# A two-layer decoder trunk: the token mixers' attention, retention and decode rows laid between projection tiles and convolution taps

## The chip, the cores and the metric

The kernel runs on one core of a Trainium2 chip, in one launch for both layers. The metric is the device time in microseconds, the median of several executions of the same program, in float32 throughout.

## The reference

The input is one prompt of 512 tokens and eight decode groups of four tokens each, 544 rows of 1024 numbers. Each of the two layers does the following, with its own weights:

```
h = x @ w_in          # 11 chunks of 256 columns:
                      # ret q,k,v,gate | dil q,k,v | conv val,gate | sgu u,v
A = layer_norm_per_head(retention(rot(q), rot(k), v)) * silu(gate)
B = dilated attention(rot(q), rot(k), v)   # prompt: own rows;
                                           # samples: 1024 cached rows as well
C = silu(layer_norm(causal_conv31(val * sigmoid(gate))))
D = gelu(u) * (lower_triangular(W_s) @ layer_norm_per_group(gelu(v)))
x = LN(alpha * x + concat(A, B, C, D) @ w_out)
x = LN(alpha * x + top-2-of-8 experts in the best of 4 groups(x))
```

Beside the final rows it returns the new retention states, the keys and values, the rows of the convolution, and the normalised v rows. A, B, C and D depend only on `h`, and not on each other.

## The kernel before, in words

One program is written for each engine, in program order, and counters (semaphores) order the engines against each other: `E.need(name, n)` makes an engine wait until `name` has been counted n times in this layer, `E.done` counts it, and `E.link` makes an engine wait for its own instruction. What stands behind a wait on the same engine waits too.

A layer has two parts. The first part, called the mixers here, is computed from x in SBUF. TensorE turns x into xT (`turn_rows`, L507), 128 rows at a time. Then come eleven projection chunks (`chunk`, L531): each is five tiles of eight matmuls, written in turn to five PSUM banks, and ScalarE moves each tile to `h` (`proj_out`, L948), with a sigmoid, gelu or silu where the chunk wants one. The order of chunks before is VAL, GATE, U, V, RG, RQ, RK, RV, SQ, SK, SV. Between them VectorE does the group norm of V (L1054) and the convolution, 62 instructions of 784 columns over a context that TensorE turned (L1103, L1106), then its norm. GpSimd multiplies VAL by GATE and rotates RQ, RK, SQ and SK (`rotate`, L1580), tile by tile and each operation by itself.

Only when all chunks are out are the queries and keys turned (L613, L617): eight groups of four transposes into xT, which x no longer needs. Then come the retention of the prompt in four steps (scores L635, products L642, rows L657 and L660, with a state in SBUF between the steps), the retention of the samples (L672 to L691), and 16 attention units (four row blocks of four heads). A unit is scores (L703) on TensorE, bias, maximum and sign on VectorE (L1205 to L1208), the exponential on ScalarE (L986), a turn of the probabilities (L787), a copy (L992), the values (L770), and the division (L1232). Cached keys and values of the samples (L731, L758) are done between units, two groups at a time, with tiles of 32 columns of the array; four buffers `kv` hold them. At last the four mixed blocks are turned (L519 once more) and multiplied by `w_out` in four chunks (L542), x + y is normalised on VectorE (L1301, L1274, L1280, L1283), and TensorE turns x again for the router's logits (L826).

The second part routes the tokens on VectorE (L1354 to L1486, with matmuls L835, L837, L843 and L848 between) and then runs the experts: blocks of 32 tokens, three lanes, matmuls L871 and L889, weights of 2 MB each loaded by `expert_load` (L431). The first loads of a layer's experts are issued behind the second out chunk.

All loads and stores stand in one queue, that of the SyncE program (L338 to L520), in program order: the ring of three weight chunks (`ring_load`, L351), kv (`kv_load`, L363), parameters, results, experts. The queue waits where its next entry waits.

The mixers' chunks and units follow each other like this in TensorE's program:

```
for c in range(5, 9):
    chunk(c, "proj", "proj_out")
...                       # turn the convolution's rows
chunk(9, "proj", "proj_out")
...                       # spatial gating
chunk(10, "proj", "proj_out")
...                       # turn queries and keys, retention, samples
for u in range(16):
    if u < 15:
        att_scores(u + 1)
    E.need("att_p", u + 1)
```

## Time and profile before

| | us |
|---|---|
| median of 3 runs (lowest, highest) | 1935.23 (1932.53, 1937.45) |
| the profiled execution's own time | 1938.98 |
| its span, first to last instruction | 1936.9 |
| TensorE busy | 1472.9 (76%) |
| VectorE busy | 544.6 (28%) |
| GpSimd busy | 398.8 (21%) |
| ScalarE busy | 208.8 (11%) |

Mean granted TensorE clock of the profiled execution: 0.854 of full speed. Moved by DMA: 532.60 MB. In the page, an engine's busy time is a union of its instructions; the lines of a timeline give start, duration, engine, line and operation, merged where instructions of one kind follow each other. A matmul in float32 shows as two instructions (x64 is four tiles of eight). Layer 1 is read for the mixers, from 982 us on, where VAL and GATE are out.

### The profile page before, as it was taken

What the parts mean: (1) busy time and instruction counts of PE and PEld (TensorE: products, weight loads), DVE (VectorE), ACT (ScalarE), POOL (GpSimd) and SP (SyncE); (2) the same over time, 40 slices, a digit from 0 to 9 for tenths busy, and PEclk for the clock granted to TensorE, in tenths of its full rate; (3) what the DMA queues carried; (4) which work ended last, traced back from release to release, by engine and by line L of the source; (5) the groups of instructions that cost most, each with busy time, mean ns of one, the idle gap of its engine ahead of it and who ended that gap; (6) DMA issues with size and microseconds to landing.
All of it is one profiled execution on the core that took longest, in us unless ns stands there. A gap on an engine that the chain in (4) does not pass through costs nothing. (4 is left out here: it accounts for less than half of the span.)

```text
span 1936.9 us, 40042 instructions
## 1 busy us (share of the span) xinstructions
PE 1472.9 (76%) x16276; PEld 1012.2 (52%) x16276; DVE 544.6 (28%) x1215; ACT 208.8 (11%) x579; POOL 398.8 (21%) x533
## 2 busy tenths in 40 slices
PE   8998899949567576767499988995766758566990
PEld 7887647835334333434488874684433424333550
DVE  0395352541000000000609735236100101000116
ACT  2111030001000000000121112201000000000010
POOL 3149230111001011100311943001211101110113
PEclk9999589969788888879699977896878878887995
DMA  8711041949999999999531102265899999999824
GB/s 341 280 66 58 1 159 64 364 173 359 428 425 382 425 426 425 384 425 386 194 135 66 44 36 109 92 256 225 333 427 425 380 427 424 426 425 425 349 89 142
DMA packets 77409, 532.60 MB, mean 275 GB/s; under 512 B 14430, under 2 KB 31770, under 8 KB 48538
## 3 DMA queue, kind: packets, MB, share of 16 engines
q1 hardware_dynamic: 45466, 482.00, 60.4%
q0 software_dynamic: 11136, 35.40, 5.0%
q10 hardware_dynamic: 20736, 14.18, 2.3%
q8 instruction: 53, 0.87, 0.2%
q14 instruction: 18, 0.15, 0.0%
HBM read 772.37 MB, written 35.98 MB: 417 GB/s over the span
## 5 line engine op out<-in xcount | busy, mean ns | idle before, releaser
L871 PE MATMUL ps<-arena,xT 128*32 128x256 f32 x6912 | 477.8, 437 | 252.1 <-DMA arena<-in_w 250.5
L871 PEld LDWEIGHTS ps<-arena,xT 128*32 128x32 f32 x6912 | 274.9, 126 | 444.7 <-issue 352.9
L542 PE MATMUL ps<-arena,xT 128*128 128x256 f32 x1920 | 424.9, 382 | 0.9 <-issue 0.9
L542 PEld LDWEIGHTS ps<-arena,xT 128*128 128x128 f32 x1920 | 363.9, 191 | 51.5 <-issue 1.0
L1496 DVE COPY xT<-ps 128x128 f32<-128x128 f32 x108 | 31.5, 291 | 907.2 <-PE ps L880 907.2
L889 PE MATMUL ps<-arena,xT 128*32 128x256 f32 x3456 | 212.2, 386 | 34.0 <-DVE xT L1496 22.4
L1674 POOL COPY xT<-xT 128x1 int32 x108 | 19.7, 182 | 805.8 <-PE ps L861 805.8
L889 PEld LDWEIGHTS ps<-arena,xT 128*32 128x32 f32 x3456 | 108.7, 110 | 110.2 <-issue 27.2
L1676 POOL DMA_INDIRECT xT<-x1d,xT x108 | 105.0, 972 | 53.1 <-POOL xT L1674 49.6
L1106 DVE SCALAR_TENSOR_TENSOR arena<-arena 128x784 f32<-128x784 f32 x120 | 113.7, 1029 | 0.0
L1017 ACT ACTIVATE xT<-ps 128x128 f32<-128x128 f32 x108 | 30.0, 278 | 668.7 <-PE ps L871 668.7
L1593 POOL TENSOR_TENSOR arena<-arena,const 128x128 f32<-128x128 f32 (+1 forms) x40 | 68.8, 1719 | 73.9 <-ACT arena L956 73.6
L1022 ACT COPY xT<-ps 128x256 f32<-128x256 f32 x108 | 40.2, 373 | 293.2 <-PE ps L889 289.6
L519 PE MATMUL ps<-const,arena 128*128 128x128 f32 (+1 forms) x240 | 37.8, 311 | 43.0 <-DVE arena L1283 32.8
L953 ACT ACTIVATE arena<-ps 128x256 f32<-128x256 f32 x88 | 33.8, 384 | 273.9 <-PE ps L542 273.9
L519 PEld LDWEIGHTS ps<-const,arena 128*128 128x128 f32 (+1 forms) x240 | 30.5, 167 | 49.6 <-DVE arena L1283 34.4
L1658 POOL TENSOR_TENSOR mv<-mv,halfc 128x1 f32<-128x1 f32 (+1 forms) x10 | 13.3, 1329 | 204.9 <-DVE mv L1307 204.9
L1492 DVE COPY xT<-ps 128x256 f32<-128x256 f32 x114 | 48.4, 425 | 24.5 <-PE ps L861 24.5
L861 PE MATMUL ps<-const,xT 128*128 128x128 f32 x228 | 44.4, 277 | 10.6 <-DMA xT<-x1d,xT 9.5
L940 ACT COPY xT<-ps 128x512 f32<-128x512 f32 (+1 forms) x50 | 24.8, 523 | 189.6 <-PE ps L519 189.4
L1060 DVE TENSOR_REDUCE pstat<-arena 128x20 f32<-128x1280 f32 (+1 forms) x4 | 5.9, 1486 | 124.1 <-ACT arena L956 124.1
L880 PEld LDWEIGHTS ps<-const,xT 128*128 128x128 f32 x108 | 14.9, 138 | 44.5 <-issue 44.5
(244 smaller groups left out, 1223.1 us busy)
## 6 DMA issues: line engine op xcount, KB each, us to landing
arena<-in_w SPq DMA_DIRECT2D x324, 2048.0 KB
arena<-in_w_proj SPq DMA_DIRECT2D x30, 1024.0 KB, 5.0
arena<-in_kv SPq DMA_DIRECT2D x32, 640.0 KB, 5.1
yd<-xT ACTq DMA_DIRECT2D x432, 32.0 KB
yd<-arena POOLq DMA_DIRECT2D x22, 512.0 KB, 18.6
rowpar<-in_rowpar SPq DMA_DIRECT2D x2, 2708.0 KB, 17.2
x1d<-arena SPq DMA_DIRECT2D x8, 512.0 KB, 14.6
arena<-x1d SPq DMA_DIRECT2D x8, 512.0 KB, 6.7
```

What stands on the lines that cost most here:

```text
L519: ins = pe.transpose(ps[g][:, j * 128:j * 128 + n], source(t, 4 * g + j), ident[0:n, 0:n])
L542: ins = pe.matmul(bank[0:n, 0:CW], xT[:, k, 128 * t:128 * t + n], ring[slot(c)][:, k, :], start=(k == 0), stop=(k == KT - 1))
L861: ins = pe.transpose(TOKENS[:, b * 128:(b + 1) * 128], xg[q][:, b * 128:(b + 1) * 128], ident)
L871: ins = pe.matmul(HB[q][r, 0:256], xgT[q][:, k % 2, BLK * (k // 2):BLK * (k // 2 + 1)], w13[q][:, :, k, 128 * j:128 * (j + 1)], start=(k = ...
L889: ins = pe.matmul(YB[q][r, 0:256], hT[q][:, BLK * c:BLK * (c + 1)], w2[q][:, c, 256 * t:256 * (t + 1)], start=(c == 0), stop=(c == 3), til ...
L953: ins = act.activation(h[0:n, c, t, :], bank[0:n, 0:CW], func.get(c, ACT.Copy))
L1022: act.copy(yo[q], YB[q][:, 0:256]).then_inc(sem(f"y_out{q}"), 1)
L1106: ins = dve.scalar_tensor_tensor(out=acc[:, cb, :], in0=src, scalar=cw[:, cb * TAPS + j:cb * TAPS + j + 1], in1=acc[:, cb, :], op0=ALU.mul ...
L1492: dve.tensor_copy(xgT[q], TOKENS[:, 0:256].rearrange("p (b m) -> p b m", b=2)).then_inc(sem(f"xgT{q}"), 1)
L1496: dve.tensor_copy(hT[q], HIDDEN[:, 0:128]).then_inc(sem(f"hT{q}"), 1)
L1593: pool.tensor_tensor(t1[:, t], a[:, t], sb_, ALU.mult)
L1676: pool.indirect_dma_start(out=xg[q], out_offset=None, in_=x1q, in_offset=bass.IndirectOffsetOnAxis(ap=gidx[q], axis=0))\
```

## The change

It does seven things in the mixers of each layer, and one in the routing.

1. Chunk order: VAL, GATE, SQ, SK, SV, RQ, RK, V, RV, U, RG. The ring is three buffers for the first three chunks and two from then on. Tiles now cycle through two PSUM banks, not five.
2. The queries and keys of the attention are turned as soon as SQ and SK are rotated, into `sT`; those of the retention later, into `rT`. Both stand on the place of x in SBUF, and so does the fourth kv buffer. In layer 1 x is therefore stored to `x2d` in HBM at the layer's start; in both layers the residual is loaded back (from the input, or from `x2d`) when `rT` is done with.
3. Each attention unit but the first has one projection tile between its scores and its turn: RQ, RK and V. Each retention step has one tile behind it (RV, RV, U, U), and the rest of U stands between the samples' steps. RG stands between the turns of the mixed rows.
4. VectorE's 62 convolution instructions are split: 26 before the rotation of SQ and SK, 12 behind it, and 24 between attention units. The norms of the convolution, of V and of the retention's rows are split in the same way, and stand between the retention's steps.
5. Engines change: the rotation of SQ and SK, the decay of RK and the retention's norm go from GpSimd to VectorE; the copies of the convolution's rows, of the attention's turned queries and keys and of QB go to ScalarE. V's gelu is one ScalarE instruction of 1280 columns behind the units. GpSimd's rotation is six whole instructions, not 22.
6. Cached keys and values go four sample groups at a time, one for each strip of 32 columns (the order of the caches is changed for it).
7. The gate of RG is applied tile by tile, and the last chunk, the turn of the mixed rows and the first out tiles overlap.
8. In the routing TensorE does 18, 28 and 4 matmuls of 256 columns, whose results nobody reads, in front of three of its waits.

```diff
-CACHES = (0, 2, 1, 3, 4, 6, 5, 7)
-VAL, GATE, U, V, RG, RQ, RK, RV, SQ, SK, SV = range(NCH)
+CACHES = (0, 2, 4, 6, 1, 3, 5, 7)
+VAL, GATE, SQ, SK, SV, RQ, RK, V, RV, U, RG = range(NCH)
+TAPS_AT = (38, 41, 44, 47, 50, 53, 54, 57, 59, 62)
...
-        kv.append(ctx_acc[:, VEXP:VEXP + 2 * NKEY])
+        QK = LANES * EXPERT - WCOLS
+        sT, rT = (arena[:, QK + 4 * NTOK * k:QK + 4 * NTOK * (k + 1)]
+                  .rearrange("p (k n) -> p k n", k=4) for k in range(2))
+        kv.append(arena[:, QK + 4 * NTOK:QK + 4 * NTOK + 2 * NKEY])
...
 # SyncE
-                sp.wait_ge(sem("x2"), L * TILES)
+                if L:
+                    for t in range(TILES):
+                        sp.wait_ge(sem("x2"), (L - 1) * TILES + t + 1)
+                        sp.dma_start(x2d[...], x[0:ROWS[t], t, :])
...
+                E.need("smp_o", 1)
+                E.need("qb_ok", 1)
+                for t in range(TILES):
+                    sp.dma_start(x[0:ROWS[t], t, :],
+                                 x2d[rows, :] if L else io["x_in"][rows, :])
...
 # TensorE
+                def tile(c, t):
+                    if t == 0:
+                        pe.wait_ge(sem(f"ring{slot(c)}"), filled(c, L))
+                    j = serial(c, t, True)
+                    if j >= 2:
+                        E.need("proj_out", j - 1)
+                    E.done(weigh(ps[2 + j % 2], c, t), "proj")
...
+                E.need("rot_s", 1)
+                E.need("ctx_out", 3)
+                turn_pair(SQ, SK, "s_tr", lambda k: ("s_act", k + 1))
+                for t in range(2, TILES):
+                    tile(SV, t)
...
+                E.need("s_act", 4)
+                E.need("proj_out", (SV + 1) * TILES)
+                att_scores(0)
+                for u in range(16):
+                    if u < 15:
+                        att_scores(u + 1)
+                    if u > 10:
+                        E.need("conv_out", u - 10)
+                    if u:
+                        tile(RQ + (u - 1) // TILES, (u - 1) % TILES)
+                    if 10 <= u < 15:
+                        turn_conv(u - 10, RQ * TILES + u - 1)
+                    att_turn(u)
+                    if u:
+                        att_values(u - 1)
+                    if u == 1:
+                        new_key_scores()
+                        cached_key_scores(range(0, NKV))
+                    if u == 3:
+                        cached_key_scores(range(NKV, NB))
...
+                tile(RV, 0)
+                att_values(15)
+                E.need("rot_r", 1)
...
+                turn_pair(RQ, RK, "r_tr", ...)
+                tile(RV, 1)
...
+                for n in range(4):
+                    E.need("ret_a", n + 1)
+                    if n < 3:
+                        ret_scores(n + 1)
+                    if n:
+                        E.need("ret_upd", n)
+                    ret_products(n)
+                    ret_rows(n)
+                    tile((RV, RV, U, U)[n], (3, 4, 0, 1)[n])
...
+                tile(RG, 0)
+                tile(RG, 1)
...
+                for t in range(2, TILES):
+                    turn_mix(t - 2)
+                    tile(RG, t)
+                turn_mix(3)
+                E.need("proj_out", 55)
...
+                def run_idle(n):
+                    for k in range(n):
+                        pe.matmul(HIDDEN[:, 0:256], ident, ones2, start=True, stop=True)
+                run_idle(18)
                 E.need("member", 1)
...
+                run_idle(28)
                 E.need("onehot", 1)
...
+                run_idle(4)
                 E.need("which", 1)
...
 # VectorE
+                taps(0, 26)
+                E.need("proj_out", (SK + 1) * TILES)
+                E.link(rotate(SQ, 8, "scos", "ssin"))
+                E.done(rotate(SK, 8, "scos", "ssin"), "rot_s")
+                taps(26, TAPS_AT[0])
...
+                attend(0)
+                for u in range(16):
+                    if u:
+                        total_inverse(u - 1)
+                    if u < 15:
+                        attend(u + 1)
+                    if u < 9:
+                        taps(TAPS_AT[u], TAPS_AT[u + 1])
...
 # GpSimd
+                    pool.tensor_tensor(t1, a, si, ALU.mult)
+                    pool.tensor_tensor(t2, b, si, ALU.mult)
+                    pool.tensor_tensor(a, a, co, ALU.mult)
+                    E.link(pool.tensor_tensor(b, b, co, ALU.mult))
+                    pool.tensor_tensor(a, a, t2, ALU.subtract)
+                    return pool.tensor_tensor(b, b, t1, ALU.add)
```

## Rows read from the trace of the kernel before

**Rows 1.** The page's shares of the chain that ended last, by line.
```profile
DMA arena<-in_w 18%; PE ps L871 6%; PE ps L542 3%; PE ps L889 1%; DMA x1d<-arena 1%; DVE arena L1528 1%; DVE arena L1280 1%; PE ps L758 1%; DVE bn L1274 0%; PE ps L770 0%; PE ps L703 0%; PE ps L731 0%; SPq L431 0%; DVE arena L1283 0%; PE ps L787 0%
```
**Rows 2.** Layer 1: stretch, us, busy (instructions) of PE PEld DVE ACT POOL, clock, DMA.
```profile
982.00:1126.00 144.00, 140.70 (x1188) 120.86 (x1188) 90.38 (x113) 24.59 (x76) 73.38 (x84) 1.00 0.18 67
1126.00:1137.00 11.00, 7.41 (x52) 5.75 (x54) 2.90 (x5) 4.31 (x8) 3.74 (x12) 0.84 0.41 156
1137.00:1174.00 37.00, 34.54 (x212) 26.02 (x210) 9.88 (x36) 1.60 (x3) 7.35 (x16) 0.52 0.00 0
1174.00:1241.00 67.00, 58.79 (x347) 32.38 (x343) 32.98 (x95) 18.85 (x53) 16.31 (x6) 0.83 0.41 145
1241.00:1249.00 8.00, 6.74 (x40) 5.29 (x40) 2.96 (x5) 2.61 (x5) 0.00 (x0) 0.79 0.00 0
```
**Rows 3.** TensorE's timeline: one projection chunk, and the next one's start.
```profile
981.82 14.08 PE L542 MATMUL ps<-arena,xT 128*128 128x256 f32 x64
996.86 14.08 PE L542 MATMUL ps<-arena,xT 128*128 128x256 f32 x64
```
**Rows 4.** TensorE's timeline: an attention unit of one block, one of four blocks.
```profile
1183.19 0.33 PE L770 MATMUL ps<-arena 128*128 128x64 f32 x2
1183.46 0.48 PE L703 MATMUL ps<-xT 64*128 64x128 f32 x2
...
1229.56 1.10 PE L770 MATMUL ps<-arena 128*128 128x64 f32 x8
1230.60 1.12 PE L703 MATMUL ps<-xT 64*128 64x512 f32 x2
1231.65 0.65 PE L787 MATMUL ps<-const,arena 128*128 128x128 f32 x4
1232.24 2.35 PE L758 MATMUL ps<-arena 128*32 128x256 f32 x20
```
**Rows 5.** TensorE's timeline: the first two calls of cached keys.
```profile
1177.91 4.48 PE L731 MATMUL ps<-arena 128*32 128x512 f32 x16
...
1184.83 2.35 PE L731 MATMUL ps<-arena 128*32 128x512 f32 x16
```
**Rows 6.** TensorE's timeline: one retention step's start and the next one's.
```profile
1141.44 1.17 PE L642 MATMUL ps<-arena 128*128 128x128 f32 x4
...
1148.63 1.22 PE L642 MATMUL ps<-arena 128*128 128x128 f32 x4
```
**Rows 7.** The convolution on VectorE; ScalarE's table; GpSimd beside VectorE, layer 1.
```profile
1030.55 56.84 DVE L1106 SCALAR_TENSOR_TENSOR arena<-arena 128x784 f32<-128x784 f32 x60
1166.89 1.28 ACT L986 ACT_TABLE_LOAD   x1
1059.88 27.82 POOL L1593 TENSOR_TENSOR arena<-arena,const 128x128 f32<-128x128 f32 x1 [36.80 <-ACT arena L956]
```
**Rows 8.** Layer 0: TensorE's third chunk, and GpSimd's VAL times GATE.
```profile
43.27 14.08 PE L542 MATMUL ps<-arena,xT 128*128 128x256 f32 x64
...
49.83 2.88 POOL L1573 TENSOR_TENSOR arena<-arena 128x1280 f32<-128x1280 f32 x1
```
**Rows 9.** SyncE's queue in layer 1: the first expert loads.
```profile
1279.84 35.86 SPq L431 DMA_DIRECT2D arena<-in_w  x8
```
**Rows 10.** The routing of layer 1: TensorE, and VectorE where it reads the counts.
```profile
1323.89 4.84 PE L826 MATMUL ps<-router_w,xT 128*128 128x40 f32 x32
1337.15 0.64 PE L835 MATMUL ps<-xT,const 128*128 128x32 f32 x2 [8.42 <-DVE xT L1387]
1348.91 4.62 PE L843 MATMUL ps<-xT 128*128 128x120 f32 x20 [9.90 <-DVE xT L1459]
1358.60 6.23 PE L871 MATMUL ps<-arena,xT 128*32 128x256 f32 x64 [0.52 <-DVE xT L1492]
1366.16 3.66 PE L871 MATMUL ps<-arena,xT 128*32 128x256 f32 x64
```

More of the change, by code:

```diff
@@ L420, in _ @@
                 E.done(sp.dma_start(out, ret_state), "stores", 16)
-                for c in range(NCH + 2, NCH + NOUT):
+                E.need("sgu_vn", 1)
+                out = io["s_sgu"][bass.ds(L, 1)].rearrange("a p c -> (a p) c")
+                E.done(sp.dma_start(out, h[0:NS, V, 4, :]), "stores", 16)
+                for c in range(NCH, NCH + NOUT):
                     ring_load(c)
@@ L688, in _ @@
-                E.need("vexp", 1)
-                for hd in range(NH):
-                    hp, hh = hd // 2, hd % 2
-                    ins = pe.matmul(ps[4 + hp][half(hh), :], h[0:NS, RK, 4, hd * HD:(hd + 1) * HD],
-                                    vexp[:, hd, :, :].rearrange("p b e -> p (b e)"), start=True, stop=True)
-                E.done(ins, "smp_o")
                 def att_scores(u):
@@ new lines, in _, with ret_scores @@
+                E.need("smp_rows", 1)
+                E.need("smp_y", 1)
+                turn_pair(RQ, RK, "r_tr", lambda k: (("r_act", "r_dve")[k % 2], k // 2 + 1))
+                tile(RV, 1)
+                def ret_scores(n):
+                    for hd in range(NH):
+                        hp, hh = hd // 2, hd % 2
+                        ins = pe.matmul(ps[4 + hh][:, hp * 128:(hp + 1) * 128], rT[half(hh), 2 + hp, n * 128:(n + 1) * 128],
+                                        rT[half(hh), hp, n * 128:(n + 1) * 128], start=True, stop=True)
+                    E.done(ins, "ret_s")
@@ new lines, in _ @@
+                E.done(ins, "smp_o1")
+                tile(U, 2)
+                E.need("ret_a", 5)
+                E.need("smp_o1c", 1)
+                for hd in range(NH):
+                    pe.matmul(ps[0][0:NS, hd * HD:(hd + 1) * HD], sm[0][0:NS, hd * NS:(hd + 1) * NS],
+                              h[0:NS, RV, 4, hd * HD:(hd + 1) * HD], start=True, stop=False)
+                    ins = pe.matmul(ps[0][0:NS, hd * HD:(hd + 1) * HD], sm[1][0:64, hd * NS:(hd + 1) * NS],
+                                    ident[0:64, 0:64], start=False, stop=True)
@@ new lines, in _ @@
+                E.need("vexp", 1)
+                for hd in range(NH):
+                    hp, hh = hd // 2, hd % 2
+                    ins = pe.matmul(ps[4 + hp][half(hh), :], h[0:NS, RK, 4, hd * HD:(hd + 1) * HD],
+                                    vexp[:, hd, :, :].rearrange("p b e -> p (b e)"), start=True, stop=True)
+                E.done(ins, "smp_o")
+                tile(U, 3)
+                tile(U, 4)
+                E.need("sgu_vn", 1)
+                E.need("sgu_w", 1)
+                wT = CP("sgu_wT").rearrange("p (g t) -> p g t", g=4)
@@ L975, in _ @@
-                E.need("qk_tr", 9)
-                E.done(act.copy(xT[:, 0:8, SEQ:NTOK], ps[0][:, 0:8 * NS].rearrange("p (k n) -> p k n", k=8)), "qk_act")
+                for t in range(TILES):
+                    turn_out(t, (0, 1))
+                    if t:
+                        proj_out(VAL, t - 1)
+                        proj_out(GATE, t - 1)
+                proj_out(VAL, TILES - 1)
+                proj_out(GATE, TILES - 1)
+                for t in range(TILES):
+                    proj_out(SQ, t)
@@ new lines, in _ @@
+                E.need("ret_s", 5)
+                for hh in range(2):
+                    dst, m = (z[0:NS, 0:NH * NS].rearrange("p (c g k) -> p c g k", c=2, g=2)[:, :, hh, :]
+                              for z in (sm[0], C("ret_mask_s")))
+                    ins = dve.tensor_tensor(dst, ps[4 + hh][0:NS, 0:2 * NS].rearrange("p (c k) -> p c k", c=2), m, ALU.mult)
+                E.done(ins, "ret_a")
+                rows, last = h[:, RQ, 0:4], h[0:NS, RQ, 4:5]
+                rows_stat, last_stat = rstat[:, 0:32], rstat[:, 32:40]
@@ new lines, in _ @@
+                for hp in range(2):
+                    ins = dve.scalar_tensor_tensor(out=s0[:, hp, :], in0=s0[:, hp, :], scalar=C("c_decay_s")[:, hp:hp + 1],
+                                                   in1=ps[4 + hp][:, :], op0=ALU.mult, op1=ALU.add)
+                E.done(ins, "smp_upd")
+                centre(last, NH, HD, last_stat)
+                spread(last, NH, HD, last_stat)
+                E.link(along(sv, RP("sgu_ln_g"), ALU.mult))
+                E.done(along(sv, RP("sgu_ln_b"), ALU.add), "sgu_vn")
```

930 lines of the change are left out of this document (465 added, 465 removed).

## The prediction

> **What bounds the kernel now.** I read the chain of waits first. Its largest line by far is the load of expert weights [rows 1]. That chain binds only while experts run; those loads are the same before and after, and a layer's expert part starts when its router is done. So whatever ends the mixers earlier moves everything behind it, by the same time in each of the two layers. The first expert loads stand in the queue behind the second out chunk [rows 9] and move with it, so no transfer holds them back.
>
> Then the stretches of the mixers in layer 1 [rows 2]. From 982 to 1249 us they take 267 us. In the first 144, projection, TensorE is busy 140.7 at the full clock (1.00). From 1126 to 1249 it is busy 107.5 of 123 us, so little of that time is idle; what is lost is the clock: 0.52 in the retention, 0.83 in the attention. VectorE is busy 139 us in all, 90 of them beside the projection, and no other engine is near a limit. TensorE in program order is the bound, partly at half speed, partly waiting for the short chain VectorE, ScalarE, TensorE of each unit.
>
> **The work that is left, at full clock.** Busy time times clock, by stretch [rows 2]: 140.7 + 7.41 x 0.84 + 34.54 x 0.52 + 58.79 x 0.83 + 6.74 x 0.79 = 140.7 + 6.2 + 18.0 + 48.8 + 5.3 = 219.0 us. Removed from it: cached keys and values in calls of four groups. Two groups in two column strips take 2.35 us at full clock, keys or values [rows 4, 5]; four in four strips should take the same, as four-strip matmuls of 256 columns do now in the experts (64 in 3.66 us, 57 ns each [rows 10], against 20 in 2.35 us, 118 ns each, in two strips [rows 4]). Eight calls become four: minus 9.4. That leaves 209.6 us.
>
> **What is moved, and whether it fits.** A chunk is 15.04 us [rows 3], a full tile 3.5. Six of the nine chunks, 90 us, now lie between units and steps. A unit of one block costs TensorE about 0.8 us and one of four blocks 2.7 (1229.56 to 1232.24) [rows 4]; with a tile in each, iterations last 4.3 to 6.2 us, and the short fifth tiles (1.0 us) make two of them 2 to 3 us.
> VectorE: a convolution instruction is 0.948 us (56.84 / 60) [rows 7]; 26 of them from about 991 end at 1016, SK is out at about 1014, the rotation (12 instructions of 160 columns, estimated 4 us) ends at 1020, as SV's second tile does: no wait. In the first ten units it has 24 x 0.948 = 22.8 us and ten sixteenths of the attention's 33.0 [rows 2], 43.4 us; TensorE has 51 in them (nine tiles 29, units 13, samples 9). VectorE stays about a tile ahead, and adding its new work (rotation 4, decay 1.5, retention norm 9, less 6 that goes to ScalarE or into fewer copies) gives 148 of 223 us. Cost nothing, covered by TensorE; without that cover each is paid in full.
> ScalarE gains copies and gets tiles between exponentials, about 2 us of work in an iteration of 4.3 or more: nothing.
> GpSimd rotates RQ behind unit 5 and RK behind unit 10; the turn of both needs it 89 us after the first unit. Its operations wait for VectorE (one of them 27.8 us, until the convolution ended [rows 7]). Bounds: 10 us a rotation, or all starved until the last tap: even then RK would end at about 76. Nothing.
> Two PSUM banks, not five: a tile needs the one before the last to be copied, 0.4 us within 3.5. Nothing.
> Queues: SyncE gets five stores of x and five loads per layer, 2.1 MB each way, some 5 us of transfer. The stores go ahead of the parameters, at about 960, where VAL x GATE needs them at 983. The loads are issued behind the samples' retention, some 27 us before the first out tile. The four cached-key loads behind unit 1 are 2.6 MB, about 7 us in the 9 before unit 3 wants them; the last four values stand behind the ring load that waits for unit 10, about 11 us before they are wanted. This is the tightest place; I take nothing, and 2 us a layer for the upper end.
>
> **Waits that I charge** (per layer, estimates): before the first unit, the last SV copies, QB's eight small copies and the table for the exponential (1.28 us [rows 7]) stand in series on ScalarE: 4.5. Before the turn of RQ and RK, the gelu of V and its table: 2.5. The two turns' own waits: 1.6 (the turning stretch now has 3.6 idle [rows 2]). Retention, where VectorE puts norms between steps: 1.6. Spatial gating waits for V's norm, behind the samples' update on VectorE: 2.6. Last RG copy: 1.1. Sum 13.9. Bounds: 0, or twice that.
> So 209.6 + 13.9 = 223.5 us where 267 were: **43.5 us off layer 1**. In layer 0, SQ's first two tiles end at 43.3 + 7.0 = 50.3, but VAL x GATE ends at 52.7 because the clearing of yd stands ahead of it [rows 8]: 2.4 lost, **41.1 off**.
>
> **The clock of what is moved.** The retention's small matmuls kept TensorE 93% busy for 37 us, and the clock stayed at 1.2 GHz [rows 2]; a step of them took 7.2 us [rows 6], so 3.6 at full clock. Behind the second step stands only the short fifth tile of RV, so two steps run nearly together. Bounds for this term: 0, or all 18.0 us a second time. I take 5 a layer, the two steps' 7.2 less what the drop comes late: nearer the low end because three full tiles lie in between, and chunks hold 1.00. **Plus 10.**
>
> The Trainium skill, "TensorE: Matmul & The Clock Gate", section on psum-queue depth-cycling, speaks against this change: a stream that goes round its PSUM banks with brief idles between groups swings between the two clock levels. The trace before goes round five banks at 1.00, so it neither bears this out nor excludes it for two. It would give the second rival's time below.
>
> **Routing.** The unread matmuls are 0.44 us each at full clock (14.08 / 32). The first 18 start at 1328.7 (1323.89 + 4.84) at the low clock, where 8.4 us are free [rows 10]; with a climb as long as in the first expert block (6.23 against 3.66, so 5 us at half speed) they end at about 1338.6, 1 us late for VectorE's counts. The 28 take 12.3 us against 9.9 free; the matmuls behind take 2.3, not 4.6. Together about 0.9 late at the indices; then the first expert block runs at full clock: 2.6 less, with its turns 2.8. Net 1.9 earlier a layer, **minus 3.8**. Bounds: 3 earlier, or, if the clock never climbs, 0.88 each: 28 of them end 15 us past the indices' need, and 18 a layer later in all.
>
> **Sum.** 43.5 + 41.1 - 10 + 3.8 = 78.4 us off 1938.98 gives 1860.6; that execution lies 3.7 above the median of the runs shown, so 1857.
>
> **Rivals.**
> (a) The overlap closes better: no fall of the clock in the retention (minus 10) and half the waits (minus 14): 1833. For it: chunks hold 1.00. Against it: five handoffs each need another engine on time. No wait at all gives 1819.
> (b) The clock swings among units and tiles as in today's attention, 0.83 [rows 2]. The sixteen units with their tiles are 85 us of work at full clock; at 0.83 they take 103, plus 18 a layer: 1892. For it: small matmuls between tiles. Against: six tenths of that work are dense tiles.
> (c) Clock and waits together: retention all at 1.2 GHz (plus 13 a layer beyond my 5) and 4 us more waits a layer: 1857 + 34 = 1891; half of that 1874. For it: 37 us of such matmuls never raised the clock.
> (d) Slower than before: the clock falls when the first unit starts, as it did at 1126, and stays at 1.2 GHz although tiles lie between. From 1034 on there are 209.6 - 52 = 158 us of work; at half speed it takes 158 more, less the 43.5: plus 114 a layer, 2160. It decides once more than 43.5 of the 158 us, 28%, run at half speed. Against: today's attention, thinner than this, is at 0.83, a third of its time low; that is the only reason to keep it.
> (e) The moves do not overlap: tiles and units take turns with the short chain still exposed (15 of the 123 us after 1126 are idle now). Then only clock and packing are won. Gain per layer 18 + 10 + 9 = 37 less the 14 of waits: 1890, inside (b) and (c).
>
> **How the numbers follow.** Chances: forecast 0.55 (own range 1842 to 1874), (a) 0.17, (b) 0.07, (c) with (e) 0.17, (d) 0.03, and 0.01 that little changes. About 0.3%, 6 us, is what a measurement of this kernel can tell from no change. Faster 0.96, same 0.01, slower 0.03. The range reaches from inside (a) to (b) and (c): 1836 to 1892; outside it are (a)'s far half, (d), and (c) with late values.
>
> **What the changed profile would show.** Right: the first out tile of layer 0 at about 270 us and the first mixers' tiles at clock 1.00; no wait of TensorE over 1 us between units but the one before the first; calls of cached keys of 32 matmuls and about 2.4 us; a granted clock of 0.9 or more from the first unit to the out chunks; the first expert block at 3.7 us. Wrong: steps of the retention that still take 7 us; TensorE waiting for kv loads at units 3 or 12; VectorE late with a unit's maximum; an index matmul that starts over 2 us after VectorE's one-hots; or expert blocks that last longer than before.

## The result, and the profile after

| | before | after |
|---|---|---|
| median of 4 runs each, us (lowest, highest) | 1936.34 (1932.53, 1937.71) | 1859.61 (1858.84, 1865.83) |
| span of the profiled execution, us | 1936.9 | 1857.0 |
| its mean granted clock | 0.854 | 0.884 |
| TensorE busy, us | 1472.9 | 1451.7 |
| VectorE busy, us | 544.6 | 561.2 |
| GpSimd busy, us | 398.8 | 280.1 |

The medians lie 77 us apart; the ratio of all runs is 0.9614, with a 95% interval of 0.9588 to 0.9639. The forecast was 1857, in a range from 1836 to 1892.

The largest line of the chain of waits is still the load of expert weights, as in [rows 1]. The page's shares by line, of the changed kernel:

```profile
DMA arena<-in_w 19%; PE ps L952 7%; PE ps L556 6%; PE ps L970 1%; DMA x1d<-arena 1%; DVE arena L1704 1%; DVE arena L1454 1%; DVE bn L1448 0%; PE ps L561 0%; SPq L452 0%; DVE arena L1457 0%; PE ps L642 0%; PE ps L660 0%; DMA arena<-yd,slots 
```

**Where the time came from.** The mixers' share is read between the same two marks in both kernels. In layer 0 the router's logits end at 353.8 us, before at 390.1: 36.3 off. In layer 1, from the end of VAL and GATE to the end of the logits, it is 943.3 to 1251.5, 308.2 us, and was 981.9 to 1328.7 [rows 10], 346.9: 38.7 off. From the logits to the first expert block it is now 28.5 us (28.9 in layer 0), before 29.9 (30.2), and the first expert block takes 5.35 us instead of 6.23 (5.30 instead of 6.04). Together about 79, and the spans differ by 79.9.

The stretches of layer 1's mixers, with the columns of [rows 2]: turn of SQ and SK, units, turn of RQ and RK, retention, samples with the last of U, RG with the turns, out chunks.

```profile
943.40:994.00 50.60, 49.19 (x414) 42.12 (x414) 40.11 (x54) 9.94 (x31) 4.35 (x3) 1.00 0.20 76
994.00:1086.00 92.00, 86.23 (x742) 65.66 (x742) 54.59 (x113) 28.36 (x93) 20.18 (x12) 0.96 0.36 134
1086.00:1096.00 10.00, 7.95 (x53) 6.95 (x53) 4.56 (x10) 4.89 (x8) 0.00 (x0) 1.00 0.26 105
1096.00:1131.50 35.50, 35.50 (x246) 29.51 (x244) 24.25 (x45) 2.40 (x8) 11.09 (x6) 0.90 0.09 33
1131.50:1151.50 20.00, 20.00 (x209) 14.41 (x208) 16.26 (x24) 3.62 (x10) 6.25 (x2) 0.83 0.43 150
1151.50:1170.30 18.80, 18.80 (x163) 16.49 (x161) 6.61 (x17) 5.37 (x13) 0.00 (x0) 1.00 0.13 47
```

Two things are to be seen. TensorE idles 1.4 + 5.8 + 2.0 = 9.2 us. And the clock, which was 0.52 in the retention and 0.83 in the attention, is 0.96 with the units and 0.90 with the retention; what is left of its falls costs 86.23 x 0.04 + 35.5 x 0.10 + 20.0 x 0.17 = 10.4 us.

TensorE's timeline of the units, layer 1; a bracket is the idle time ahead and what ended it:

```profile
994.71 0.49 PE L642 MATMUL ps<-arena 64*128 64x128 f32 x4 [1.11 <-ACT arena L1033]
998.15 0.48 PE L652 MATMUL ps<-const,arena 128*128 128x128 f32 x1 [2.95 <-ACT arena L1076]
...
999.28 5.96 PE L556 MATMUL ps<-arena,xT 128*128 128x256 f32 x16
...
1008.86 3.72 PE L556 MATMUL ps<-arena,xT 128*128 128x256 f32 x16
...
1018.26 2.36 PE L690 MATMUL ps<-arena 128*32 128x512 f32 x32 [0.85 <-DMA arena<-in_kv]
...
1038.34 0.41 PE L652 MATMUL ps<-const,arena 128*128 128x128 f32 x2 [1.26 <-DVE arena L1283]
...
1093.52 1.09 PE L617 MATMUL ps<-const,arena 128*128 128x128 f32 x8 [1.81 <-ACT arena L1103]
```

The first unit pays its chain on ScalarE, and the tile behind takes 5.96 us instead of 3.72, because the clock fell in the wait: number 7 keeps TensorE busy there, and the tile is fast. A call of cached keys is 32 matmuls in 2.36 us, against 16 in 2.35 [rows 5]. The retention, same view:

```profile
1109.43 0.71 PE L787 MATMUL ps<-arena 128*128 128x128 f32 x4
...
1112.79 1.71 PE L561 MATMUL ps<-arena,xT 128*32 128x64 f32 x64
1114.43 1.23 PE L780 MATMUL ps<-arena 64*128 64x128 f32 x8
1115.59 1.13 PE L787 MATMUL ps<-arena 128*128 128x128 f32 x4
...
1119.36 5.41 PE L556 MATMUL ps<-arena,xT 128*128 128x256 f32 x16
...
1139.16 2.50 PE L842 MATMUL ps<-arena 32*64 32x512 f32 x8
1141.60 6.48 PE L556 MATMUL ps<-arena,xT 128*128 128x256 f32 x16
```

Products are at full clock (0.71 us, not the 1.17 of [rows 6]). The clock falls behind the second step, where only RV 4 stands between, and once more behind the samples' small matmuls. Layer 0, the two places where it waits longer, for VAL x GATE and for V's norm:

```profile
52.87 1.09 PE L596 MATMUL ps<-const,arena 128*128 128x128 f32 x8 [1.25 <-POOL arena L1749]
...
251.33 1.99 PE L853 MATMUL ps<-arena 128*128 128x256 f32 x8 [2.30 <-DVE arena L1202]
```

And the routing of layer 1, beside [rows 10]: the unread matmuls (L908) fill most of the waits, and the indices take 2.38 us instead of 4.62, but the block that follows three short waits is at half speed for a while again.

```profile
1251.40 8.83 PE L908 MATMUL ps<-const 128*128 128x256 f32 x36
1260.06 0.30 PE L914 MATMUL ps<-xT,const 128*128 128x32 f32 x2
...
1272.92 2.38 PE L923 MATMUL ps<-xT 128*128 128x120 f32 x20
...
1279.97 5.35 PE L952 MATMUL ps<-arena,xT 128*32 128x256 f32 x64 [0.52 <-DVE xT L1668]
```

### The profile page after: what moved, and what is told of

It reads as the page before. It is cut to its first block and busy times, and to the rows that moved or that the text cites. A ratio compares the mean times of both kernels' runs of the same rounds, so it can differ in the third digit from the quotient of the medians.

```text
span 1857.0 us, 40383 instructions
## 1 busy us (share of the span) xinstructions
PE 1451.7 (78%) x16476; PEld 1015.8 (55%) x16476; DVE 561.2 (30%) x1233; ACT 218.4 (12%) x615; POOL 280.1 (15%) x347
## 5 line engine op out<-in xcount | busy, mean ns | idle before, releaser
L556 PE MATMUL ps<-arena,xT 128*128 128x256 f32 x1920 | 448.8, 392 | 0.4 <-ACT arena L1033 0.4
L556 PEld LDWEIGHTS ps<-arena,xT 128*128 128x128 f32 x1920 | 370.2, 196 | 67.9 <-issue 14.7
L970 PEld LDWEIGHTS ps<-arena,xT 128*32 128x32 f32 x3456 | 109.3, 110 | 108.4 <-issue 28.6
L1810 POOL COPY xT<-xT 128x1 int32 x108 | 19.6, 182 | 804.7 <-PE ps L942 804.5
L1231 DVE SCALAR_TENSOR_TENSOR arena<-arena 128x784 f32<-128x784 f32 x120 | 122.2, 1084 | 0.0
L534 PEld LDWEIGHTS ps<-const,arena 128*128 128x128 f32 (+1 forms) x240 | 29.8, 162 | 43.5 <-DVE arena L1457 32.9
L908 PE MATMUL ps<-const 128*128 128x256 f32 x200 | 45.9, 388 | 0.0
L908 PEld LDWEIGHTS ps<-const 128*128 128x128 f32 x200 | 38.5, 195 | 5.7
L1794 POOL TENSOR_TENSOR mv<-mv,halfc 128x1 f32<-128x1 f32 (+1 forms) x10 | 13.2, 1318 | 169.6 <-DVE mv L1483 169.6
```

What stands on the lines that cost most here:

```text
L534: ins = pe.transpose(ps[g][:, j * 128:j * 128 + n], source(t, 4 * g + j), ident[0:n, 0:n])
L556: ins = pe.matmul(bank[0:n, 0:CW], xT[:, k, 128 * t:128 * t + n], ring[slot(c)][:, k, :], start=(k == 0), stop=(k == KT - 1))
L908: pe.matmul(HIDDEN[:, 0:256], ident, ones2, start=True, stop=True)
L970: ins = pe.matmul(YB[q][r, 0:256], hT[q][:, BLK * c:BLK * (c + 1)], w2[q][:, c, 256 * t:256 * (t + 1)], start=(c == 0), stop=(c == 3), til ...
L1231: ins = dve.scalar_tensor_tensor(out=acc[:, cb, :], in0=src, scalar=cw[:, cb * TAPS + j:cb * TAPS + j + 1], in1=acc[:, cb, :], op0=ALU.mul ...
```

## The experiments

Differences are between medians, against 1859.6 for the changed kernel unless another is named; a ratio is against the kernel before, and its interval is about 0.0025 (5 us) either way. So a few us are read from the traces, not from the times. A trace is one execution, though, and the same place differs between them: in the nine kernels that leave VAL x GATE of layer 0 alone (the changed one, numbers 1 to 3 and 5 to 9), TensorE's wait for it is 0.57 to 3.26 us, and in the 14 layers traced with a wait of 2.95 us before the first unit's turn, the tile behind takes 4.95 to 6.56 us. A difference of that size at such a place is not yet the edit's.

**1. The tiles ahead of the units.** RQ, RK and V are whole chunks again, and all taps stand ahead of the units. The second call of cached keys and its loads move back by a unit with them; the rest of the change stays.

```diff
+                for c in (RQ, RK, V):
+                    for t in range(TILES):
+                        tile(c, t)
                 att_scores(0)
...
-                    if u:
-                        tile(RQ + (u - 1) // TILES, (u - 1) % TILES)
```

> The changed kernel with the fifteen tiles of RQ, RK and V and all taps of the convolution put back ahead of the first attention unit (the loads of cached keys and the second call of cached keys move with them, by a unit). Everything else stays, the packing and the tiles between retention steps too. Main theory (TensorE's program order is the bound; the tiles hide each unit's chain and hold the clock): three chunks are 45.1 us, attention by itself was 67 us before and loses 9.4 by packing, 58 + 45 = 103 against some 92 to 97 now: plus 8 to 13 us a layer, plus 16 to 26 in all, and a granted clock near 0.83 in the units. Rival (the time was won elsewhere, by packing and around the retention): within 5 us of the changed kernel.

1895.6 us, ratio 0.9786 (0.9761 to 0.9810): 36 slower, more than the 16 to 26 expected, and far from the rival. Windows (the chunks, then the units) and two lines of TensorE's timeline:

```profile
1013.54:1058.60 45.06, 45.06 (x391) 39.05 (x384) 20.74 (x22) 7.21 (x24) 22.51 (x12) 1.00 0.22 74
1058.60:1135.00 76.40, 59.72 (x414) 37.82 (x403) 31.11 (x97) 28.44 (x76) 0.00 (x0) 0.78 0.34 131
```
```profile
1063.29 0.48 PE L650 MATMUL ps<-const,arena 128*128 128x128 f32 x1 [4.13 <-ACT arena L1078]
...
1078.92 4.44 PE L688 MATMUL ps<-arena 128*32 128x512 f32 x32 [4.69 <-DMA arena<-in_kv]
```

The bare units run at 0.78, and TensorE idles 16.7 of 76.4 us. Of this 6.8 are waits for cached keys and values (4.69 here, 2.11 later), which the expectation had not counted: the second four loads are issued behind the first call in both kernels, and the tiles give them time. From the first scores to the last values the units take 69 us here without the tile of RV among them, in the kernel before 63, with four calls more.

**2. The retention alone.** RV 1 to 4 and all of U stand ahead of the turn.

```diff
+                for t in range(1, TILES):
+                    tile(RV, t)
+                for t in range(TILES):
+                    tile(U, t)
                 turn_pair(RQ, RK, "r_tr", ...)
...
-                    tile((RV, RV, U, U)[n], (3, 4, 0, 1)[n])
```

> The changed kernel with RV 1 to 4 and U 0 to 4 taken from between the retention steps and put ahead of the turn of RQ and RK. Main theory (small matmuls with nothing dense between them stay at 1.2 GHz): the retention takes 37 us as before, the nine tiles 26.4, the turn 6: 69 against 57 us now, plus 12 a layer, plus 24 in all; steps of 7.2 us again, clock near 0.52. Rival (the clock fell before because of the wait ahead of the retention, and a full chunk ahead of it keeps it up): steps at 3.6 to 4 us, 51 to 55 us for the stretch, so 4 to 12 us faster in all.

1913.0 us, ratio 0.9872 (0.9846 to 0.9898): 53 slower, twice the main theory's 24. Windows (tiles, turn and first step, the rest of retention and samples), and TensorE's timeline:

```profile
1119.00:1146.60 27.60, 27.60 (x251) 23.94 (x249) 0.42 (x2) 6.49 (x14) 0.00 (x0) 1.00 0.11 39
1146.60:1159.40 12.80, 5.58 (x56) 4.58 (x50) 10.49 (x14) 2.30 (x7) 1.18 (x1) 0.94 0.00 0
1159.40:1194.00 34.60, 30.02 (x172) 22.20 (x172) 22.81 (x44) 1.60 (x3) 14.11 (x6) 0.50 0.01 3
```
```profile
1159.34 1.23 PE L783 MATMUL ps<-arena 64*128 64x128 f32 x8 [4.75 <-DVE arena L1346]
...
1200.83 3.78 PE L851 MATMUL ps<-arena 128*128 128x256 f32 x8 [6.98 <-DVE arena L1198]
```

Nine tiles at 1.00 ahead of it did not keep the clock up: behind a stretch with 7.2 us of idle time, the last 4.75 of them in one piece, it stayed at 0.50 for 35 us, although TensorE was busy 87% of them. That refutes the rival's second half and shows that the small matmuls do not raise the clock. What makes it fall is not separated here, since the wait stands there too; the changed kernel itself shows a fall without a wait, at 1112.79, and number 8 bears on it. The size was wrong since VectorE's norms, placed between steps, now stand bare (4.75 and 6.98 us): the tiles cover them too. Added, the first two experiments cost 89 us, more than the 77 of the whole change: each lays bare waits that the kernel before did not have (loads there, norms here), so they are no measure of a part's share.

**3. Cached groups in pairs**, in the changed kernel.

```diff
-CACHES = (0, 2, 4, 6, 1, 3, 5, 7)
+CACHES = (0, 2, 1, 3, 4, 6, 5, 7)
...
-                        cached_key_scores(range(0, NKV))
+                        cached_key_scores((0, 1))
+                        cached_key_scores((2, 3))
```

> The changed kernel with each call of four groups of cached keys or values split into two calls of two groups in two column strips, one behind the other at the same place. Main theory (TensorE bound; a call costs 2.35 us with two groups as with four): four more calls a layer, plus 9.4 a layer, plus 18.8 in all. Rival (the calls lie beside waits of TensorE that would be there anyway): plus 0 to 6.

1876.8 us, ratio 0.9681 (0.9656 to 0.9705): 17.2 slower, against 18.8 by the main theory; the wait for cached keys (0.85 us in layer 1, 0.83 in layer 0) is gone under the longer calls, which makes up the difference. Work on TensorE is on the path here.

**4. Packing alone, in the kernel before.**

```diff
-                    if u in (0, 2, 4, 6):
+                    if u in (0, 4):
                         cached_key_scores(u)
```

> The kernel before with the calls of four groups alone (units 0, 4, 11 and 14), nothing interleaved. Main theory: 9.4 us a layer less work, minus 18.8 in all, if it were all on the path; but the calls also covered the units' short chain there, so between minus 10 and minus 18. Rival (without tiles between units the chain VectorE, ScalarE, TensorE takes the place of the removed calls): minus 0 to 8.

1937.0 us, ratio 1.0003 (0.9985 to 1.0022): nothing, the rival's end. Of the four calls in layer 1, two wait for their loads and run at half speed behind the wait, as TensorE's timeline shows:

```profile
1190.49 4.50 PE L731 MATMUL ps<-arena 128*32 128x512 f32 x32 [2.94 <-DMA arena<-in_kv]
...
1227.85 4.49 PE L758 MATMUL ps<-arena 128*32 128x256 f32 x40 [2.35 <-DMA arena<-in_kv]
```

The first call was slow before too [rows 5], and the third took 2.37. The two waits are 5.3 us and the half speed costs 4.3, together about the 9.4 that packing should save. So the packing is worth 17 us with the tiles and none without, as the loads stood; whether loads placed otherwise would change that was not run.

**5. No unread matmuls** in the routing (`run_idle` returns at once).

> The changed kernel without the unread matmuls of the routing. Main theory: the matmuls for the counts start some 1 us earlier, those of the indices take 4.6 instead of 2.4 us and the first expert block 6.2 instead of 5.3: 1.4 + 0.9 us later per layer, plus 3 to 5 us in all. Rival (the routing ends with VectorE's chain and the indirect loads, the clock of the few matmuls doesn't count): 0 to plus 1, first expert block as late as now after the logits (28.5 us).

1867.4 us, ratio 0.9649 (0.9626 to 0.9673): 7.8 slower, above the main theory's 3 to 5, with intervals that just overlap. From the logits to the first block it took 29.2 us instead of 28.5, and the block 6.00 instead of 5.35; in layer 0 30.05 instead of 28.9. That is 2.5 us, or 2.2 with layer 0's block (4.96 instead of 5.30). Most of the rest lies ahead of anything removed: layer 0's mixers were 4.7 us longer, with a wait for VAL x GATE of 2.55 us, not 1.25, and a lower clock behind it. What the unread matmuls bring is 2.2 to 2.5 us by the trace; the time alone doesn't settle it.

**6. Two ScalarE pieces later.**

```diff
 # ScalarE: the block of QB's copies goes from ahead of the units to
                     E.done(act.copy(pT[u % 2][:, 0:n], ...), "att_pT")
+                    if u == 0:
+                        ...            # QB's eight copies
...
-                E.done(act.activation(h[:, V], h[:, V], ACT.Gelu_apprx_tanh), "v_act")
                 ...                    # copies of the turned RQ and RK
+                proj_out(RV, 1)
+                E.done(act.activation(h[:, V], h[:, V], ACT.Gelu_apprx_tanh), "v_act")
```

> The changed kernel with two pieces of ScalarE's program moved: QB's eight copies (1.8 us) behind unit 0's copy of the turned probabilities, and V's gelu with its table (2.55 us) behind the copies of the turned RQ and RK. Main theory (ScalarE's order makes these two waits): the wait before unit 0's turn falls from 2.95 to about 1.1 us, the one in the turn of RQ and RK from 1.8 to under 0.5, and the tile behind unit 0 takes 3.7 instead of 6.0: 4 to 6 us a layer, minus 8 to 12 in all. Rival (the clock falls all the same, or VectorE is late with V's norm and the waits come back behind the retention): minus 0 to 4.

1851.9 us, ratio 0.9575 (0.9553 to 0.9598): 7.7 faster, just short of the main theory's 8; the slowest of its runs (1854.4) is below the fastest of the changed kernel (1858.8). TensorE's timeline, layer 1:

```profile
995.56 0.33 PE L652 MATMUL ps<-const,arena 128*128 128x128 f32 x1 [1.49 <-ACT arena L1062]
...
996.53 5.07 PE L556 MATMUL ps<-arena,xT 128*128 128x256 f32 x16
...
1090.43 1.24 PE L617 MATMUL ps<-const,arena 128*128 128x128 f32 x8 [0.29 <-ACT arena L1101]
```

The two waits are 1.49 instead of 2.95 us and 0.29 instead of 1.81: 3.0 a layer, of which 0.4 comes back in a longer wait for cached keys (1.25). The clock still fell behind two waits of 1.1 and 1.5 us: the tile behind unit 0 takes 5.07, within the 4.95 to 6.56 of the kernels with the long wait, so that part of the main theory did not come.

**7. Unread matmuls in three waits.**

```diff
                 E.need("s_act", 4)
+                unread(ps[1], 2)
...
+                    if u == 0:
+                        unread(ps[1], 6)
                     att_turn(u)
...
+                    if t == 3:         # before the router's turn of tile 3
+                        unread(ps[7], 4)
```

> The changed kernel with unread matmuls (0.22 or 0.44 us each) in three waits of a layer: two before the first scores, six before unit 0's turn, four before the fourth row tile of the router's turn. They end no wait, they only keep TensorE busy in it. Main theory (the clock falls behind these waits, and that costs more than some of them): the tile behind unit 0 takes 3.7 instead of 6.0 us, the last two tiles of logits 1.9 each way instead of 3.5 and 4.8 for two: 2.3 + 3.5 us a layer, minus 8 to 12 in all. Rival (the clock falls also behind such matmuls, or the fill ends late): within 2 us of the changed kernel or slower.

1852.1 us, ratio 0.9570 (0.9543 to 0.9598): 7.5 faster, short of the main theory's 8 to 12 and outside the rival's 2. Its slowest run (1858.7) is just below the changed kernel's fastest. TensorE's timeline, layer 1:

```profile
999.85 3.72 PE L556 MATMUL ps<-arena,xT 128*128 128x256 f32 x16
...
1144.96 2.63 PE L860 MATMUL ps<-arena 128*128 128x256 f32 x8 [2.30 <-DVE arena L1214]
...
1240.60 1.88 PE L906 MATMUL ps<-router_w,xT 128*128 128x40 f32 x16
1242.41 0.69 PE L534 MATMUL ps<-const,arena 32*128 32x32 f32 x8
1243.02 3.01 PE L906 MATMUL ps<-router_w,xT 128*128 128x40 f32 x32
```

The tile behind unit 0 is at full clock; it is in all six layers traced with such a fill (numbers 7, 10 and 11, the last two with number 6's shorter wait as well) and in none of the 16 without (the changed kernel, numbers 2, 3, 5, 6, 8, 9 and 12). The logits took 1.88 and 3.01 us instead of 3.48 and 4.84: 2.2 + 4.6 us with the turns. But the tile U 3, 6.48 us in the changed kernel, is now 3.72, and a wait of 2.30 for V's norm stands in its place. In the changed kernel the slow tile had hidden it in layer 1; in layer 0, where that tile was fast, it showed. That the fills made this tile fast isn't shown: number 5, without them, had 3.72 and 2.30 there as well. What holds is the trade between the two, 5.00 and 1.01 us in number 9.

**8. Tiles dealt out otherwise around the retention.**

```diff
-                    tile((RV, RV, U, U)[n], (3, 4, 0, 1)[n])
+                    for c, t in (((RV, 3),), ((RV, 4), (U, 0)), ((U, 1),), ((U, 2),))[n]:
+                        tile(c, t)
```

> The changed kernel with the tiles around the retention dealt out otherwise: U 0 goes with the short RV 4 behind the second step, so that no two steps have only a short tile between them; each later tile moves one place up and RG 0 goes ahead of the spatial gating. Main theory (two steps with only 1.1 us of dense work between them bring the clock down at 1112 us): no row of the retention at half speed until the third step, 3 to 4 us a layer, minus 6 to 8 in all. Rival (the clock falls with the retention's small matmuls wherever the tiles stand, or waits for VectorE take its place): within 3 us of the changed kernel.

1862.6 us, ratio 0.9632 (0.9608 to 0.9656): no gain. TensorE's timeline of the third step's products and the tiles behind: no fall behind the second step, but one behind the samples' small matmuls:

```profile
1121.62 0.71 PE L787 MATMUL ps<-arena 128*128 128x128 f32 x4
...
1124.98 3.72 PE L556 MATMUL ps<-arena,xT 128*128 128x256 f32 x16
...
1147.31 5.64 PE L556 MATMUL ps<-arena,xT 128*128 128x256 f32 x16
```

One such trace proves little, since the place varies: number 12, which leaves these tiles alone, had no fall there in layer 1 either (RV 4 in 1.10 us). All traces together bear the theory out. With the tiles as in the changed kernel (that one, numbers 1, 3, 5 to 7, 9, 10 and 12) RV 4 or the tile behind the next step was slow in 15 of 18 layers; with them dealt out this way (8 and 11) in none of four, and in all four a fall came behind the samples' small matmuls instead. The time is the rival's.

Layer 1 won 3.3 us from the turn to the out chunks (79.6 to 76.4); layer 0 was 2.5 us longer, with a wait of 3.1 us for VAL x GATE, which the edit doesn't touch. It stays open whether this edit brings 3 us or none.

**9. GpSimd's rotation behind the convolution.**

```diff
+                E.need("conv_done", 2)
                 E.link(rotate(RQ, 32, "rcos", "rsin"))
```

> The changed kernel with GpSimd's rotation of RQ held back until VectorE's convolution is done (RK's behind it, as now). Main theory (the two engines hold each other up where both work in the arena): VectorE's three taps beside unit 7 take 2.9 us again instead of 6.35, the wait of 1.3 us before unit 7's turn goes, GpSimd's operations take 1.5 us each instead of 2.2 where VectorE has other work, and the turn of RQ and RK still finds both rotated: minus 1 to 3 us in all, seen in the trace rather than in the time. Rival (the taps were slow for another reason, or the rotation comes too late for the turn): taps of 6 us again, or a new wait of TensorE for GpSimd before the turn, 0 to plus 10.

1858.5 us, ratio 0.9607 (0.9585 to 0.9630): 1.1 faster, which no time can tell. First the changed kernel's VectorE (convolution, L1231) and GpSimd (rotation), then the same place here, VectorE's timeline and TensorE's wait:

```profile
1022.33 2.92 DVE L1231 SCALAR_TENSOR_TENSOR arena<-arena 128x784 f32<-128x784 f32 x3
...
1030.99 1.55 POOL L1768 TENSOR_TENSOR arena<-arena,const 128x640 f32<-128x640 f32 x1
1031.46 6.35 DVE L1231 SCALAR_TENSOR_TENSOR arena<-arena 128x784 f32<-128x784 f32 x3
1032.48 2.28 POOL L1769 TENSOR_TENSOR arena<-arena,const 128x640 f32<-128x640 f32 x1
```
```profile
1032.88 2.92 DVE L1231 SCALAR_TENSOR_TENSOR arena<-arena 128x784 f32<-128x784 f32 x3
...
1148.39 1.99 PE L853 MATMUL ps<-arena 128*128 128x256 f32 x8 [1.01 <-DVE arena L1202]
```

Apart, the taps took 2.92 us and the rotation 1.53 to 1.55 an instruction, and the wait before unit 7 went. Layer 0 is alike (6.40 against 2.92). So the two engines do hold each other up here; in layer 1 TensorE then met 1.01 us of V's norm instead, and little was won.

**10. Combined.** Numbers 6 and 7 (with two, three and four unread matmuls), and two edits for waits that they leave or uncover: V's norm ahead of the samples' norm, and in layer 0 the clearing of yd behind VAL x GATE.

```diff
 # VectorE
                 scaled(sv, ng, HD, pstat, 2)
+                E.link(along(sv, RP("sgu_ln_g"), ALU.mult))
+                E.done(along(sv, RP("sgu_ln_b"), ALU.add), "sgu_vn")
                 E.need("smp_o", 1)
...
 # GpSimd, behind "glu" and "sgu_w" instead of ahead of them
+                if L == 0:
+                    for k in range(CLEARS):
+                        ...
```

> The changed kernel with what the runs before pointed to: QB's copies and V's gelu later on ScalarE, unread matmuls in the waits that are left (two, three, four), V's norm finished ahead of the samples' norm on VectorE, and in layer 0 the clearing of yd behind VAL times GATE on GpSimd. Main theory (waits and the clock behind them add up, as they lie at different places): 7.7 for ScalarE's order, 5 for the fill of the logits, 1.5 to 3 for VAL times GATE, 1 to 2 for V's norm: 1843 to 1847 us. Rival (they share one slack, the first to go takes the gain of the others): about 1850, as with either alone.

1831.0 us, ratio 0.9475 (0.9448 to 0.9502): 28.6 faster than the changed kernel, 105 than the one before. More than expected (1843 to 1847). TensorE's matmuls of the spatial gating, layer 0 and layer 1, no longer wait:

```profile
240.96 1.99 PE L860 MATMUL ps<-arena 128*128 128x256 f32 x8
...
1127.48 1.99 PE L860 MATMUL ps<-arena 128*128 128x256 f32 x8
```

The logits end 13.9 us earlier in layer 0, and layer 1's mixers are 13.2 us shorter (295.0 against 308.2). Its clock there is 1.00 except in the retention (0.89).

**11. Combined, with numbers 8 and 9 added.**

> The kernel of the run before it with two more parts: the tiles of the retention dealt out so that U 0 goes with the short RV 4, and GpSimd's rotation of RQ held back until the convolution is done. Main theory: the clock stays at its upper level through the retention steps, which took 3.3 us off that stretch, and the wait before unit 7 goes: 3 to 8 us less than the run before it. Rival (the clock falls later instead, behind the samples' retention, as it did with the tiles alone): the same within 3 us.

1829.9 us, ratio 0.9464 (0.9443 to 0.9486): the same as number 10 within what can be told, as the rival had it.

**12. The two new edits of number 10 alone.**

> The changed kernel with the two parts of the combined kernels that had not run alone: in layer 0 the clearing of yd behind VAL times GATE on GpSimd, and V's norm ahead of the samples' norm on VectorE. Theory one (each part wins its own wait and the clock behind it): TensorE's wait of 1.3 to 3.1 us for VAL times GATE in layer 0 and the 1.7 us of half speed behind it go, and the wait of 2.3 us before the spatial gating too: minus 5 to 9 us in all, so that with 7.7 and 7.5 of the other two most of the 28.6 us of the combined kernel is a plain sum. Theory two (the parts only pay together, because a wait left over still brings the clock down): minus 0 to 4 us.

1852.2 us, ratio 0.9567 (0.9542 to 0.9592): 7.4 faster, inside theory one's 5 to 9. TensorE's timeline of layer 0: the turn of VAL x GATE and the gating without a wait.

```profile
49.97 1.04 PE L596 MATMUL ps<-const,arena 128*128 128x128 f32 x8
...
248.79 1.99 PE L853 MATMUL ps<-arena 128*128 128x256 f32 x8
```

Layer 0's logits end 4.2 us earlier. Layer 1's mixers are 4.9 shorter, although the changed kernel had no wait for V's norm there: a slow U 3 stood in its place, and the fall behind the second step, which the edit doesn't touch, was absent. So not all of the 7.4 is shown to be the edit's.

Alone the parts give 7.7 + 7.5 + 7.4 = 22.6, together 28.6. The difference would fit number 7, where V's norm took back 2.3 us in layer 1; but three differences known to a few us each leave room for chance.

## Why the prediction was right, point by point

**The bound and the whole.** TensorE's program order was the bound: an extra 9.4 us of its work a layer cost 17.2 us in all, 18.8 less the 1.7 of a wait that it filled (number 3). The mixers' sum was 43.5 + 41.1 - 10 = 74.6; measured 36.3 + 38.7 = 75.0. The routing was to give 3.8; measured 1.3 to 1.4 a layer ahead of the first block, and 0.7 and 0.9 in the block: 4.3. Two misses cancel in it: the index matmuls were to end 0.9 us later and ended 1.0 earlier (layer 1), and the block with its turns was to give 2.8. The prediction's own terms (18 x 0.44 and 2.6 for the climb) also put the end of the first 18 at 1339.2, not 1338.6; VectorE's counts were hardly kept waiting, as TensorE reached them 8.6 us after the logits, before 8.4.

**Packing, minus 9.4 a layer.** Right, 2.36 us a call, but only under the tiles (number 4). Rival (e), which credited the packing without overlap, had that term wrong: two of the four calls there waited for loads, and ran slow behind it.

**Waits, 13.9 a layer.** Too much: TensorE idles 9.2 us in layer 1. Before the first unit it is 1.11 + 2.95 = 4.1 (charged 4.5), before the turn of RQ and RK 1.81 (charged 2.5), by ScalarE's order in both cases (number 6). The two turns' own waits were 0.7 (charged 1.6), no retention step waited (1.6), nor the last RG copy (1.1). The 2.6 for V's norm were right in layer 0 (2.30) and nothing in layer 1, since the tile ahead ran at half speed. Not charged and there: 0.85 for cached keys, 1.26 before unit 7.

**The clock, plus 5 a layer.** Too little: 10.4 in layer 1. The place named, the steps around RV 4, was right (number 8). Missed were the tile behind the first unit's wait (2.2 us, which number 7 won back) and U 3 behind the samples' matmuls (2.8). So the forecast hit because 13.9 + 5 = 18.9 is near 9.2 + 10.4 = 19.6: the two were mis-sized in opposite directions. That they cancel so closely is luck, though they are partly the same slack, as number 7 showed.

**Layer 0, 2.4 lost to VAL x GATE behind the clearing of yd.** Right in kind and about in size: 1.25 of wait, and 8.86 instead of 7.17 us for the next two tiles. In the other traces that wait is 0.57 to 3.26.

**"Cost nothing."** GpSimd's rotation did cost something: beside it VectorE's taps took 3.4 us more, and TensorE waited 1.3 us at unit 7 in each layer. Queues: a load of cached keys or values landed in 7.8 us by the median of all 32, before in 5.1; those behind unit 1 cost 0.85 a layer, where I had taken nothing and allowed 2. The rest held.

**The rule on PSUM banks.** Chunks that now go round two banks run at a granted clock of 1.00 (64 matmuls in 14.08 us, the 45.06 us of number 1). The Trainium skill, "TensorE: Matmul & The Clock Gate", section on psum-queue depth-cycling, tells of a stream whose engine idles briefly between its groups. Here it did not idle (45.06 busy of 45.06 us), so this trace shows only that going round two banks is not enough to make the clock swing; with such idles between them no run here tests it. Rival (b)'s 0.83 stood nowhere among units with tiles; the units without them had 0.78 (number 1).

**The signs.** Right: layer 0's first out tile at 272.6, calls of 2.4 us, 1.00 in the first tiles. Wrong: a wait for cached keys at unit 3 (0.85), a wait of over 1 us between units (unit 7), 0.83 at the samples and the last of U, and a first expert block of 5.35 us, not 3.7: the unread matmuls end before three waits of 0.28, 1.31 and 0.52 us, and the clock was down again.

**The rivals.** (a) asked for half the waits and no fall of the clock in the retention, 1833. The changed kernel had neither; number 10 comes to 1831, but partly by other means: its clock still falls in the retention (0.89), and it also holds the logits' gain, which (a) did not count. (c) and (e) wanted more waits than there were; (d), half speed throughout, did not occur.

## What to carry to other kernels

Dense, independent work put between the links of a short chain paid three times here: it hides the chain, it holds TensorE's clock, and it gives loads and norms of other engines their time. Packing the small work brought nothing until that cover was there. Then look for what each engine does just ahead of a handoff, move it behind, and test the moves together, since a wait that one of them leaves can take the gain of the others.

## What was unexpected

- VectorE's taps and GpSimd's elementwise instructions hold each other up in both directions: 6.35 us against 2.92 for three taps, up to 2.28 against 1.54 for an instruction on GpSimd. The Trainium skill, "GPSIMD Engine Reference", section 1, says that GpSimd shares its SBUF interfaces with VectorE, and names VectorE instructions with two SBUF inputs as a case of contention; a tap is such an instruction, and number 9 agrees. Not every overlap showed it: the three rotation instructions ahead took 1.54 to 1.55 us beside shorter VectorE work, and in the kernel before GpSimd alone paid: one instruction of 27.8 us, beside taps of 0.95 [rows 7].
- TensorE 87% busy with small matmuls stayed at 0.50 for 35 us behind a stretch of 12.8 us with 7.2 idle, with 27 us of tiles at 1.00 ahead of that (number 2).
- Waits as short as 1.1 and 1.5 us, close together, were followed by a tile partly at the lower clock (5.07 us, number 6); where unread matmuls filled the waits it took 3.72 (number 7).
- A slow clock can hide a late engine: where the tile U 3 ran at full speed, TensorE waited 2.30 us behind it for VectorE's norm, and where it took 6.48 us it did not wait (number 7). So both have to go for either to count.
- Where the clock falls is not the same in every execution: with the same tiles around it, the fall at the retention's second step came in 15 of 18 layers (number 8). One trace before and one after do not show what an edit did to it.
